# A fourth buffer for the gate matrices of the last layer's experts

## The chip, the cores and the metric

The kernel runs on one core of a Trainium2 chip. The metric is the device time of one execution in microseconds (us). The kernel before took 1708.57 us, the median of 3 runs (1705.90, 1708.57 and 1712.19).

## What is computed

A backbone of two layers over 256 latent tokens and 256 context tokens, of 1024 numbers each, all in float32. Each layer does: a normed and modulated input, three token mixers from one projection, a merge, an output projection, a residual; then the mixture of experts, which is where the change is:

```python
def grouped_moe(h, router_w, router_b, w_gate, w_up, w_down):
    ...                                   # top 2 of 16 experts for each token
    for e in range(N_EXPERTS):            # 16
        he = jax.nn.silu(h @ w_gate[e]) * (h @ w_up[e])
        out = out + combine[..., e:e + 1] * (he @ w_down[e])
    return out
```

`w_gate[e]` and `w_up[e]` are 1024 by 512, `w_down[e]` is 512 by 1024: 2 MB each, 6 MB for an expert, 96 MB for a layer, and each is used once. The last layer (layer 1) works on the 256 latent tokens alone.

## The kernel before, in words

The kernel gives each expert its tokens: the router's choice becomes lists of tokens, the rows of an expert's tokens are gathered from a copy of the tokens in HBM (`moe_rows`), turned, multiplied by gate and up, turned again, multiplied by down. In the last layer each expert has room for 64 tokens in the main loop, and the results are summed by TensorE in PSUM. An expert of the last layer has these steps on TensorE, in this order for expert i: its gate product (L1361, 32 matmuls), the sum of expert i-2's results (L1404), the turn of expert i-1's hidden rows (L1369), its up product (L1361, 32 matmuls), the turn of expert i+1's rows (L1351), the turn of a table of weights (L1394), and the down product of expert i-1 (L1379, 16 matmuls).

**Where the matrices go.** Each of the three matrices has a small set of buffers ("ways") in the on-chip memory. `WAYS[l]` (line 52) is how many for gate, up and down in layer l: 3, 3 and 3 in the last layer. Expert i's matrix uses buffer i modulo the count. Buffer 0 is a slot of the `ring` of weights, the others are pieces of other tensors (`more_sets`, line 389): for gate in the last layer, buffer 1 is half of `residual` and half of `ret_tab`, buffer 2 is `hT`. `expert_parts` (line 783) gives the pieces of a buffer and `expert_tile` (line 839) issues one DMA for each piece. A gate or up matrix has 16 KB in a row for each of 128 partitions, so a piece of a quarter has rows of 4 KB.

**What sets the order.** SyncE (SP) issues all weight transfers from one queue, in the order of its program. In the last layer it first issues the matrices of experts 0, 1 and 2 at places fixed by hand; then the loop at line 958 runs over the experts: for step i it waits until expert i's gate product is done and issues the gate of expert i + 3, waits for expert i's up product and issues the up of expert i + 3, waits for expert i-1's down product and issues the down of expert i + 2. The order in the queue is therefore gate, up, down, gate, up, down. After the loop SP issues the final gain row.

GpSimd has its own queue: a gather of the first experts' rows (L2400), four small scatters that write the lists of tokens (`slot_tokens`, L2422, 12 in the whole kernel with the eight of the first layer), a read of the lists, and then a gather for each expert.

The pieces of memory named by the change are parts of `arena`, a tensor that many stages share: columns 12288 and 13312 hold the tokens' rows `h_tok` that the product `first_rows` reads to make the first expert's rows (it ends by raising `moe.rowsT`), 7168 a modulation row, 18432 tables of the router.

Of the kernel before, what the change touches and what calls it, by code (L numbers as in the profile page):

```python
# [17 lines left out]
ALU = mybir.AluOpType  # L18
# [7 lines left out]
D = 1024  # L26
# [15 lines left out]
EXPERTS = 16  # L42
# [5 lines left out]
TILE = KD * COLS  # L48
CAPS = ((P,) * 4 + (96,) * 6 + (64,) * 6, (64,) * EXPERTS)
RUN = ((0, 1, 10, 2, 4, 11, 3, 12, 5, 6, 7, 8, 9, 13, 14, 15), tuple(range(EXPERTS)))  # L50
FIXED = 2
WAYS = ((3, 3, 2), (3, 3, 3))
CHIP = (3, EXPERTS)
POOL_TILES = 2
MARK_IN = 4
# [62 lines left out]
def first_tile(l):  # L118

    return 0 if l < DEPTH - 1 else XT  # L120
# [129 lines left out]
def trunk(nc, x, c, ctx, c_ctx, w_ada, b_ada, norm_mix_g, norm_ffn_g, w_in, diff_lambda, diff_subln_g,  # L250
# [22 lines left out]
    with ExitStack() as stack:  # L273
        def sb(name, cols, dt=F32):
            return stack.enter_context(nc.sbuf_tensor(name, [P, cols], dt))

        def sem(name):
            return stack.enter_context(nc.semaphore(name))


        res_flat = sb("residual", NT * D)[:, :]
        res = res_flat.rearrange("p (t d) -> p t d", t=NT)
        hT_flat = sb("hT", KD * TOK)[:, :]
# [3 lines left out]
        ret_flat = sb("ret_tab", RT_H * 2 * TAB)[:, :]  # L287
# [3 lines left out]
        NCOL = DEPTH + DEPTH * KB  # L291
        p_col = sb("p_col", NCOL)
# [46 lines left out]
        def region(at, n):  # L339
            assert at + n <= ARENA  # L340
            return arena[:, at:at + n]
# [31 lines left out]
        def mod_rows(l, g, n=1):  # L373
# [13 lines left out]
        junk2 = region(17920, 512).bitcast(BF16)  # L387
        big = lambda at: [region(at, 2 * TILE)]
        more_sets = (([big(20992), [hT_flat]], [big(3072), [region(16384, TILE), ret_flat[:, 0:TILE]]], [big(7168)]),
                     ([[res_flat[:, 0:TILE], ret_flat[:, 0:TILE]], [hT_flat]], [big(8192), big(3072)], [big(20992), big(14336)]))  # L390

        rows_e, rowsT_of = region(0, D), (chunks(1024, KD, P), chunks(1024, KD, MORE))
        y_bufs = ((region(2048, D), region(11264, D)), (region(2048, 512), region(2560, 512)))
# [23 lines left out]
        PC_SUB, PC_GN = 0, DEPTH  # L417
# [4 lines left out]
        param_in, x_in, const_in, ret_in = sem("param_in"), sem("x_in"), sem("const_in"), sem("ret_in")  # L422
        ctx_in, gains_in = sem("ctx_in"), sem("gains_in")
        slot_in = [sem(f"slot{s}_in") for s in range(RING)]
        expert_in = [[sem(f"expert_{name}{way}_in") for name in ("gate", "up", "down")] for way in range(max(max(w) for w in WAYS))]
        ada_ready = sem("ada_ready")
        ident_in, cond_in, bias_in = sem("ident_in"), sem("cond_in"), [sem(f"bias{n}_in") for n in range(4)]
        rows_zeroed, mods_row = sem("rows_zeroed"), sem("mods_row_ready")
        eps_set = sem("eps_set")
        cols_turned, cols_kept, cols_scaled = sem("cols_turned"), sem("cols_kept"), sem("cols_scaled")  # L430
        cond_ready, lam_ready = sem("cond_ready"), sem("lam_ready")
        lam_exp, gam_ready = sem("lam_exp"), sem("gam_ready")
        mods_a = sem("mods_a_ready")
# [15 lines left out]
        h2_ready, h2_out, h2_turned = sem("h2_ready"), sem("h2_out"), sem("h2_turned")  # L449
# [12 lines left out]
        moe = Moe(sem, "moe")  # L462
# [4 lines left out]
        nq = [NT - first_tile(l) for l in range(DEPTH)]  # L467
# [8 lines left out]
        def before(counts, l):  # L476
            return sum(counts[:l])
# [242 lines left out]
        def multiplied(key):  # L720
# [9 lines left out]
            if kind == "out":  # L730
                return wo_ready, 2 * before(nq, l + 1)
            return (moe.gate, moe.up, moe.down)[j], EXPERTS * l + max(i for i in range(EXPERTS) if i % WAYS[l][j] == 0) + 1

# [49 lines left out]
        def expert_parts(l, i, j):  # L783

            k = KF if j == 2 else KD
            if i % WAYS[l][j] == 0:
                return [expert_slot(expert_slots[l][j], k)]
            parts = more_sets[l][j][i % WAYS[l][j] - 1]
            return [part.rearrange("p (k c) -> p k c", k=k // len(parts)) for part in parts]
# [4 lines left out]
        def weights_in(l, i, j):  # L794
            same = lambda m, upto: sum(len(expert_parts(m, n, j)) for n in range(upto) if n % WAYS[m][j] == i % WAYS[l][j])
            return 16 * (sum(same(m, EXPERTS) for m in range(l)) + same(l, i + 1))
# [23 lines left out]
        def _(sp):  # L820
# [20 lines left out]
            def expert_tile(l, i, j, e):  # L841

                at = 0
                for part in expert_parts(l, i, j):
                    k = part.shape[1]
                    if j == 2 and in_pairs(cap_of(l, i)):
                        to, of = part.rearrange("p (h j) c -> p h (j c)", j=2), pairs_v[l, e][:, at // 2:(at + k) // 2, :]
                    else:
                        to, of = part, (gate_v, up_v, down_v)[j][l, e][:, at:at + k, :]
                    sp.dma_start(to, of).then_inc(expert_in[i % WAYS[l][j]][j], 16)  # L850
                    at += k
# [21 lines left out]
            for l in range(DEPTH):  # L873
# [80 lines left out]
                chosen = {2: expert_of(2)}  # L954
                expert_tile(l, 2, 0, chosen[2])
                if l == 0:
                    expert_tile(l, 2, 1, chosen[2])
                for i in range(EXPERTS):
                    ahead, later = i + WAYS[l][0], i - 1 + WAYS[l][2]
                    if ahead < EXPERTS:  # L960
                        chosen[ahead] = expert_of(ahead)
                        sp.wait_ge(moe.gate, EXPERTS * l + i + 1)
                        expert_tile(l, ahead, 0, chosen[ahead])
                        sp.wait_ge(moe.up, EXPERTS * l + i + 1)
                        expert_tile(l, ahead, 1, chosen[ahead])
                    if i >= 1 and later < EXPERTS:
                        sp.wait_ge(moe.down, EXPERTS * l + i)
                        expert_tile(l, later, 2, chosen.pop(later))
# [524 lines left out]
        def _(act):  # L1493
# [45 lines left out]
            for l in range(DEPTH):  # L1539
# [96 lines left out]
                def keep_o(b, j):  # L1636
                    act.wait_ge(o_turned, 2 * KB * l + KB * (b == 0) + j + 1)
                    bank = bank_of(l, banked[l].index(("turn_o", j))) if b == 2 else 2 + j
                    src, dst = ps[:, bank, P * t0:TOK], oT[b][:, j, P * t0:TOK]
                    if (l, b, j) == (0, 2, 0):  # L1640
                        act.wait_ge(cols_scaled, 1)
                    if b == 2:
                        ins = act.activation(dst, src, ACT.Copy, scale=p_col[:, PC_GN + KB * l + j:PC_GN + KB * l + j + 1])  # L1643
                    else:
                        ins = act.activation(dst, src, ACT.Copy, scale=p_col[:, PC_SUB + l:PC_SUB + l + 1])
                    ins.then_inc(oT_ready, 1)
# [147 lines left out]
        def _(dve):  # L1794
# [6 lines left out]
            def mixers_constants():  # L1801

                dve.wait_ge(const_in, 16)
                dve.tensor_copy(tri_ones[:, :], cst[:, C_TRI:C_TRI + 2 * P + 2 * NT])
                dve.wait_ge(param_in, 16 * PARAMS)
                lv = lam_in.rearrange("p (n a d) -> p n a d", a=2, d=HD)
                lt = lam_t.rearrange("p (n d) -> p n d", d=HD)
                step(dve.tensor_tensor(lt, lv[:, :, 0, :], lv[:, :, 1, :], ALU.mult))
                step(dve.tensor_reduce(lam[:, 0:4], lt, AX.X, ALU.add))

                dve.scalar_tensor_tensor(out=lgwork[:, 0, :], in0=loggam[:, :], scalar=-1.0, in1=loggam[:, :],
                                         op0=ALU.mult, op1=ALU.min).then_inc(lam_ready, 1)
                dve.wait_ge(lam_exp, 2)
                for l in range(DEPTH):
                    init = 0.8 - 0.6 * math.exp(-0.3 * l)
                    dve.scalar_tensor_tensor(out=lam[:, 8 + l:9 + l], in0=lam[:, 5 + 2 * l:6 + 2 * l], scalar=-init,
                                             in1=lam[:, 4 + 2 * l:5 + 2 * l], op0=ALU.add, op1=ALU.subtract)

                e_, s_, s2, acc = (lgwork[:, i, :] for i in (1, 2, 3, 0))
                step(dve.tensor_scalar(s_, e_, 2.0, None, ALU.add))  # L1820
                step(dve.reciprocal(s_, s_))
                step(dve.tensor_tensor(s_, s_, e_, ALU.mult))
                step(dve.tensor_tensor(s2, s_, s_, ALU.mult))
                step(dve.tensor_scalar(acc, s2, 1.0 / 17, None, ALU.mult))
                for n in range(7, 0, -1):
                    step(dve.scalar_tensor_tensor(out=acc, in0=acc, scalar=1.0 / (2 * n + 1), in1=s2,
                                                  op0=ALU.add, op1=ALU.mult))
                step(dve.scalar_tensor_tensor(out=acc, in0=acc, scalar=1.0, in1=s_, op0=ALU.add, op1=ALU.mult))
                step(dve.tensor_scalar(acc, acc, 2.0, None, ALU.mult))
                dve.scalar_tensor_tensor(out=loggam[:, :], in0=loggam[:, :], scalar=0.0, in1=acc,  # L1830
                                         op0=ALU.min, op1=ALU.subtract).then_inc(gam_ready, 1)
                dve.wait_ge(cols_kept, 1)
                for l in range(DEPTH):
                    init = 0.8 - 0.6 * math.exp(-0.3 * l)
                    step(dve.tensor_scalar(p_col[:, PC_SUB + l:PC_SUB + l + 1], p_col[:, PC_SUB + l:PC_SUB + l + 1],
                                           0.5 * (1.0 - init), None, ALU.mult))
                dve.tensor_scalar(p_col[:, PC_GN:NCOL], p_col[:, PC_GN:NCOL], 0.5, None, ALU.mult).then_inc(cols_scaled, 1)

            def modulation(l, g):

# [35 lines left out]
            for l in range(DEPTH):  # L1876
# [298 lines left out]
                at = 0  # L2175
# [326 lines left out]
```

## Time and profile before

| | us |
|---|---|
| median of 3 runs | 1708.57 |
| lowest, highest | 1705.90, 1712.19 |
| the profiled execution | 1709.88 |
| its span | 1708.2 |
| TensorE busy in the span | 1618.7 (95%) |
| VectorE, ScalarE busy | 522.2, 316.2 |
| mean granted TensorE clock | 0.985 of full speed |
| moved by DMA | 370.52 MB, mean 217 GB/s |

The profile is of one execution; the durations below are from it. A busy share is a mean over the whole span: what bounds the last layer's experts must be read from their own stretch, which starts near 1460 us (the first gate product) and ends near 1700 us. The DMA share of a stretch is the mean over 16 DMA engines.

### The profile page before, as it was taken

What the parts mean: (1) busy time and instruction counts of PE and PEld (TensorE: products, weight loads), DVE (VectorE), ACT (ScalarE), POOL (GpSimd) and SP (SyncE); (2) the same over time, 40 slices, a digit from 0 to 9 for tenths busy, and PEclk for the clock granted to TensorE, in tenths of its full rate; (3) what the DMA queues carried; (4) which work ended last, traced back from release to release, by engine and by line L of the source; (5) the groups of instructions that cost most, each with busy time, mean ns of one, the idle gap of its engine ahead of it and who ended that gap; (6) DMA issues with size and microseconds to landing.
All of it is one profiled execution on the core that took longest, in us unless ns stands there. A gap on an engine that the chain in (4) does not pass through costs nothing.

```text
span 1708.2 us, 21387 instructions
## 1 busy us (share of the span) xinstructions
PE 1618.7 (95%) x9005; PEld 988.9 (58%) x9005; DVE 522.2 (31%) x1210; ACT 316.2 (19%) x715; POOL 64.6 (4%) x68
## 2 busy tenths in 40 slices
PE   5999988999999999988999998999999998999987
PEld 2765634744444436854546655776678887555543
DVE  1232365522433112431111115345534314211112
ACT  2121233211111100110011013234312201100001
POOL 0000000000000000020000013000000000100000
PEclk8999999999999999999999999999999999999999
DMA  9463412233424447289999995432124366999996
GB/s 371 185 222 148 148 37 83 55 112 104 156 91 168 159 144 287 81 214 396 408 391 392 400 357 204 136 99 74 38 75 147 117 236 267 346 389 392 395 386 267
DMA packets 118863, 370.52 MB, mean 217 GB/s; under 512 B 6722, under 2 KB 83580, under 8 KB 96236
## 3 DMA queue, kind: packets, MB, share of 16 engines
q1 hardware_dynamic: 109516, 344.70, 54.8%
q0 software_dynamic: 4400, 13.69, 2.4%
q10 hardware_dynamic: 4848, 10.73, 2.0%
q8 instruction: 73, 1.20, 0.3%
q14 instruction: 26, 0.21, 0.0%
HBM read 356.40 MB, written 12.69 MB: 216 GB/s over the span
## 4 chain that ended last, share of the span: by engine, by line
PE 81%; DMA 8%; DVE 4%; SPq 2%; ACT 2%; POOL 1%; issue 1%; ACTq 0%; DVEq 0%; POOLq 0%
PE ps L1221 15%; PE ps L1361 12%; PE ps L1094 11%; PE ps L1097 9%; PE ps L1018 8%; PE ps L1238 7%; PE ps L1379 6%; PE ps L1031 3%; DMA ring<-in_w_exp_gate 3%; SPq L850 2%; PE ps L1129 1%; DMA arena<-moe_rows,idx_all 1%; PE ps L1124 1%; PE ps L1351 1%; PE ps L1404 1%; PE ps L1147 1%
## 5 line engine op out<-in xcount | busy, mean ns | idle before, releaser
L1221 PE MATMUL ps<-hT,ring 128*128 128x512 f32 (+1 forms) x768 | 262.3, 491 | 1.4 <-ACT arena L1643 1.4
L1094 PE MATMUL ps<-hT,ring 128*128 128x512 f32 (+1 forms) x544 | 209.7, 538 | 0.0
L1221 PEld LDWEIGHTS ps<-hT,ring 128*128 128x128 f32 x768 | 142.5, 190 | 115.2 <-issue 105.8
L1097 PE MATMUL ps<-ring,hT 128*128 128x256 f32 (+1 forms) x832 | 175.3, 368 | 5.1 <-DVE arena L1919 4.0
L1097 PEld LDWEIGHTS ps<-ring,hT 128*128 128x128 f32 x832 | 148.0, 192 | 36.1 <-issue 18.6
L1094 PEld LDWEIGHTS ps<-hT,ring 128*128 128x128 f32 x544 | 101.2, 191 | 97.7 <-issue 92.7
L1238 PE MATMUL ps<-arena,ring 128*128 128x512 f32 (+1 forms) x384 | 133.4, 487 | 0.0
L1361 PE MATMUL ps<-ring,arena 128*64 128x256 f32 (+2 forms) x928 | 117.1, 377 | 5.6 <-DMA ring<-in_w_exp_gate 3.1
L1361 PE MATMUL ps<-arena 128*64 128x256 f32 (+2 forms) x1008 | 99.6, 355 | 3.8 <-DMA arena<-in_w_exp_up 2.7
L1238 PEld LDWEIGHTS ps<-arena,ring 128*128 128x128 f32 x384 | 72.3, 190 | 51.5 <-issue 46.7
L1361 PEld LDWEIGHTS ps<-ring,arena 128*64 128x64 f32 (+2 forms) x928 | 67.3, 136 | 53.1 <-issue 34.1
L1018 PE MATMUL ps<-ring,arena 128*128 128x256 f32 x384 | 84.3, 381 | 1.6 <-DVE arena L2088 1.5
L1361 PEld LDWEIGHTS ps<-arena 128*64 128x64 f32 (+2 forms) x1008 | 60.8, 130 | 37.5 <-issue 16.9
L1018 PEld LDWEIGHTS ps<-ring,arena 128*128 128x128 f32 x384 | 72.5, 190 | 13.4 <-DVE arena L2088 2.8
L1379 PE MATMUL ps<-arena 128*64 128x512 f32 (+2 forms) x352 | 76.3, 558 | 4.0 <-issue 2.6
L1611 ACT ACTIVATE arena<-ps,st 128x512 f32<-128x512 f32 (+1 forms) x96 | 58.2, 612 | 81.5 <-DVE st L1981 44.3
L1379 PE MATMUL ps<-ring,arena 128*64 128x512 f32 (+2 forms) x352 | 66.4, 522 | 0.2 <-issue 0.2
L2087 DVE SCALAR_TENSOR_TENSOR arena<-arena,ps 128x512 f32<-128x512 f32 (+1 forms) x32 | 17.7, 555 | 154.4 <-PE ps L1238 154.4
L2283 DVE COPY arena<-ps 128x256 f32<-128x256 f32 (+2 forms) x32 | 15.4, 482 | 159.4 <-PE ps L1369 159.4
L1031 PE MATMUL ps<-ring,cond 128*32 128x512 f32 x384 | 55.3, 669 | 9.3 <-DMA ring<-in_w_ada 7.3
L2293 DVE TENSOR_TENSOR arena<-arena,ps 128x256 f32<-128x256 f32 (+2 forms) x32 | 20.9, 653 | 141.4 <-PE ps L1361 141.4
L1652 ACT ACTIVATE arena<-ps 128x512 f32<-128x512 f32 (+1 forms) x48 | 23.5, 490 | 219.0 <-PE ps L1221 219.0
(258 smaller groups left out, 1535.4 us busy)
## 6 DMA issues: line engine op xcount, KB each, us to landing
ring<-in_w_in SPq DMA_DIRECT2D x54, 1024.0 KB, 6.2
ring<-in_w_ada SPq DMA_DIRECT2D x48, 1024.0 KB, 7.1
arena<-in_w_exp_down SPq DMA_DIRECT2D x18, 2048.0 KB, 23.9
arena<-in_w_exp_up SPq DMA_DIRECT2D x15, 2048.0 KB, 24.2
ring<-in_w_exp_down SPq DMA_DIRECT2D x14, 2048.0 KB, 20.7
ring<-in_w_exp_gate SPq DMA_DIRECT2D x12, 2048.0 KB, 23.6
ring<-in_w_exp_up SPq DMA_DIRECT2D x12, 2048.0 KB, 23.8
hT<-in_w_exp_gate SPq DMA_DIRECT2D x10, 2048.0 KB, 22.6
```

The costliest lines, as they stand in the source:

```text
L850: sp.dma_start(to, of).then_inc(expert_in[i % WAYS[l][j]][j], 16)
L1018: last = pe.matmul(dst, a, b, start=(i == 0), stop=(i == len(pairs) - 1))
L1031: last = pe.matmul(ps[32 * c:32 * (c + 1), 7, :], cond[:, k, :], slot(n)[:, 512 * c:512 * (c + 1)], start=(k == 0), stop=(k == KD - 1))
L1094: last = pe.matmul(ps[:, bank, 0:tok.stop - tok.start], w[:, k, at:at + width], hT[:, k, tok], start=(k == 0), stop=(k == KD - 1))
L1097: last = pe.matmul(ps[:, bank, 0:width], hT[:, k, P * tok:P * (tok + 1)], w[:, k, at:at + width], start=(k == 0), stop=(k == KD - 1))
L1221: last = pe.matmul(ps[:, 0, lo:TOK], kview(n)[:, k, P * (m % 2):P * (m % 2 + 1)], hT[:, k, lo:TOK], start=(k == 0), stop=(k == KD - 1))
L1238: last = pe.matmul(ps[:, 1, lo:TOK], wide(n)[:, k, P * (m % 2):P * (m % 2 + 1)], oT[BRANCH_ORDER[b_n]][:, k, lo:TOK], start=(k == 0), stop ...
L1361: last = pe.matmul(ps[wid * i:wid * (i + 1), bank, col:col + cols], rowsT_of[l][:, j, at:at + wid], w[j][:, cols * i:cols * (i + 1)], star ...
L1379: last = pe.matmul(ps[wid * i:wid * (i + 1), Y_AT[l] + p + half, 0:cols], hidT_of[l][:, block, wid * side:wid * (side + 1)], w[j][:, cols ...
L1611: ins = act.activation(prob[:, g % 2, 512 * j:512 * j + nk], ps[:, 2 + j, 0:nk], ACT.Exp, bias=s[:, 2 + j:3 + j], scale=SCALE, accum_out=s ...
L1652: act.activation(sig[:, v % 2, P * t0:TOK], ps[:, 0, P * t0:TOK], ACT.Tanh, scale=0.5).then_inc(sig_ready, 1)
L2293: return dve.tensor_tensor(out, a, b, ALU.mult)
```

## The change

`WAYS` for the last layer goes from (3, 3, 3) to (4, 3, 3). A fourth gate buffer is made of four pieces of 1024 columns of `arena`. Before the loop SP waits until all tokens' rows are ready and until the first expert's rows are made, and issues expert 3's gate as four DMAs of 512 KB. In the loop the gate that is issued is that of expert i + 4, and the up has its own counter (`above`, expert i + 3 as before). One semaphore (`cols_scaled`) is joined with another (`cols_kept`), and the list of the weights' semaphores has a fourth entry for gate alone. Experts 3, 7, 11 and 15 use the new buffer, 1, 5, 9 and 13 the one in two pieces.

```diff
-WAYS = ((3, 3, 2), (3, 3, 3))
+WAYS = ((3, 3, 2), (4, 3, 3))
...
-                     ([[res_flat[:, 0:TILE], ret_flat[:, 0:TILE]], [hT_flat]], [big(8192), big(3072)], [big(20992), big(14336)]))
+                     ([[res_flat[:, 0:TILE], ret_flat[:, 0:TILE]], [hT_flat], [region(at, D) for at in (12288, 13312, 7168, 18432)]], [big(8192), big(3072)], [big(20992), big(14336)]))
...
+                if WAYS[l][0] > 3:
+                    sp.wait_ge(h2_ready, before(nq, l + 1))
+                    sp.wait_ge(moe.rowsT, EXPERTS * l + 1)
+                    chosen[3] = expert_of(3)
+                    expert_tile(l, 3, 0, chosen[3])
                 for i in range(EXPERTS):
-                    ahead, later = i + WAYS[l][0], i - 1 + WAYS[l][2]
+                    ahead, above, later = i + WAYS[l][0], i + WAYS[l][1], i - 1 + WAYS[l][2]
                     if ahead < EXPERTS:
                         chosen[ahead] = expert_of(ahead)
                         sp.wait_ge(moe.gate, EXPERTS * l + i + 1)
                         expert_tile(l, ahead, 0, chosen[ahead])
+                    if above < EXPERTS:
                         sp.wait_ge(moe.up, EXPERTS * l + i + 1)
-                        expert_tile(l, ahead, 1, chosen[ahead])
+                        expert_tile(l, above, 1, chosen[above])
                     if i >= 1 and later < EXPERTS:
                         sp.wait_ge(moe.down, EXPERTS * l + i)
                         expert_tile(l, later, 2, chosen.pop(later))
...
-                        act.wait_ge(cols_scaled, 1)
+                        act.wait_ge(cols_kept, 2)
...
-                dve.tensor_scalar(p_col[:, PC_GN:NCOL], p_col[:, PC_GN:NCOL], 0.5, None, ALU.mult).then_inc(cols_scaled, 1)
+                dve.tensor_scalar(p_col[:, PC_GN:NCOL], p_col[:, PC_GN:NCOL], 0.5, None, ALU.mult).then_inc(cols_kept, 1)
```

## Rows read from the trace of the kernel before

**Rows 1.** Page, 40 equal slices of the span: busy tenths of TensorE and the DMA engines.

```profile
PE   5999988999999999988999998999999998999987
DMA  9463412233424447289999995432124366999996
```

**Rows 2.** Stretches: length, busy us of PE, PEld, DVE, ACT, POOL, PEclk, DMA share, GB/s.

```profile
1460.00:1609.00 149.00, 147.11 (x1064) 77.12 (x1064) 24.01 (x53) 15.06 (x34) 12.25 (x14) 0.99 1.01 379
1609.00:1693.00 84.00, 72.64 (x502) 40.77 (x502) 12.38 (x27) 5.79 (x14) 2.66 (x3) 1.00 0.97 382
```

**Rows 3.** Chain that ended last, from 1633 us: start us, us, what.

```profile
1633.70 43.22 DMA ring<-in_w_exp_gate
1677.05 3.67 PE ps L1361 x32
```

**Rows 4.** Timeline of SP's issues, experts 14 and 15: start us, us, engine, line, out<-in.

```profile
1626.17 4.83 SPq L850 DMA_DIRECT2D arena<-in_w_exp_up  x1
1631.05 2.60 SPq L850 DMA_DIRECT2D arena<-in_w_exp_down  x1
...
1638.08 3.07 SPq L850 DMA_DIRECT2D ring<-in_w_exp_up  x1
...
1659.14 0.38 SPq L850 DMA_DIRECT2D ring<-in_w_exp_down  x1
```

**Rows 5.** DMA issues, us to landing last: those issued at 1626.17, 1631.05, 1633.70, 1638.08.

```profile
arena<-in_w_exp_up SPq DMA_DIRECT2D x1, 2048.0 KB, 40.9
...
arena<-in_w_exp_down SPq DMA_DIRECT2D x1, 2048.0 KB, 41.0
...
ring<-in_w_exp_gate SPq DMA_DIRECT2D x1, 2048.0 KB, 43.2
...
ring<-in_w_exp_up SPq DMA_DIRECT2D x1, 2048.0 KB, 43.7
```

**Rows 6.** Timeline of TensorE, experts 14 and 15; in brackets idle before and its end.

```profile
1667.18 3.67 PE L1361 MATMUL ps<-arena 128*64 128x256 f32 x32 [0.45 <-DMA arena<-in_w_exp_up]
...
1672.11 3.65 PE L1379 MATMUL ps<-arena 128*64 128x512 f32 x16 [0.25 <-issue]
...
1682.94 3.67 PE L1361 MATMUL ps<-ring,arena 128*64 128x256 f32 x32
```

**Rows 7.** Timeline of SP's issues at the start: expert 2's gate, expert 3's gate and up.

```profile
1447.04 0.33 SPq L850 DMA_DIRECT2D hT<-in_w_exp_gate  x1
1465.44 0.33 SPq L850 DMA_DIRECT2D ring<-in_w_exp_gate  x1
1469.59 0.33 SPq L850 DMA_DIRECT2D ring<-in_w_exp_up  x1
```

**Rows 8.** DMA issues: us to landing of the issues at 1447.04, 1465.44, and an earlier one at 1435.60.

```profile
hT<-in_w_exp_gate SPq DMA_DIRECT2D x1, 2048.0 KB, 21.6
...
ring<-in_w_exp_gate SPq DMA_DIRECT2D x1, 2048.0 KB, 14.2
...
ring<-in_w_exp_up SPq DMA_DIRECT2D x1, 2048.0 KB, 7.5
```

**Rows 9.** Stretches as in rows 2: both layers' list scatters, and just after the last layer's.

```profile
1466.00:1476.00 10.00, 9.20 (x84) 5.75 (x86) 1.45 (x4) 0.98 (x2) 0.59 (x1) 1.00 1.00 175
1476.00:1486.00 10.00, 10.00 (x80) 5.44 (x78) 1.91 (x4) 0.87 (x2) 0.93 (x1) 1.00 1.00 410
750.00:766.00 16.00, 15.10 (x42) 7.01 (x41) 1.90 (x4) 1.19 (x2) 4.52 (x6) 1.00 0.99 154
```

**Rows 10.** DMA by size of packet, 930 to 940 us: first layer, many 4 KB rows.

```profile
DMA packets 646, 3.91 MB, mean 391 GB/s; under 512 B 58, under 2 KB 58, under 8 KB 510
```

**Rows 11.** Page, DMA issues: pieces of 512 KB, and the gate matrices in two pieces.

```profile
ring<-in_w_branch SPq DMA_DIRECT2D x24, 512.0 KB, 3.6
...
residual<-in_w_exp_gate SPq DMA_DIRECT2D x5, 1024.0 KB, 23.8
ret_tab<-in_w_exp_gate SPq DMA_DIRECT2D x5, 1024.0 KB, 27.5
```

More of the change, by code:

```diff
@@ L424, in trunk @@
         slot_in = [sem(f"slot{s}_in") for s in range(RING)]
-        expert_in = [[sem(f"expert_{name}{way}_in") for name in ("gate", "up", "down")] for way in range(max(max(w) for w in WAYS))]
+        expert_in = [[sem(f"expert_{name}{way}_in") for name in ("gate", "up", "down")[0:sum(max(w[j] for w in WAYS) > way for j in range(3))]]
+                     for way in range(max(max(w) for w in WAYS))]
         ada_ready = sem("ada_ready")
@@ L429, in trunk @@
         eps_set = sem("eps_set")
-        cols_turned, cols_kept, cols_scaled = sem("cols_turned"), sem("cols_kept"), sem("cols_scaled")
+        cols_turned, cols_kept = sem("cols_turned"), sem("cols_kept_and_scaled")
         cond_ready, lam_ready = sem("cond_ready"), sem("lam_ready")
```

## The prediction, made before the change was run

> **What bounds the kernel now.** I read the slices of the page first, then stretches of the last layer's experts, then the chain of waits, and last the single transfers. The slices show TensorE near full nearly everywhere, and two places where the DMA engines are full too: the experts of the two layers [rows 1]. For the last layer the stretches split in two. From 1460 to 1609 us TensorE works 147.1 of 149 us; from 1609 to 1693 it works 72.6 of 84, so 11.4 us are idle, while the DMA share stays near 1 in both [rows 2]. TensorE is ahead of the transfers at the start, loses that lead and then waits. The chain says the same: it goes through the transfer of the last gate, issued at 1633.70 and landed 43.2 us later, to the gate product at 1677.05 [rows 3, 5]. A transfer of 2 MB that lands 43 us after its issue is not short of a buffer. 43.2 us at 390 GB/s are 16.8 MB, or eight matrices ahead of it in the queue.
>
> An expert brings 6 MB, 6.29 million bytes, 16.1 us at the 390 GB/s that I take from rows 10 (391). TensorE needs about 14.0: 5.89 us from a gate product to its up product (1677.05 to 1682.94, no idle), 4.6 to 4.7 from there to the down product (1667.18 to 1672.11, less 0.25 of idle), and 3.5 for that [rows 3, 6]. So the queue is the bound, by some 2.1 us an expert, and what counts is when each place in the queue lands, and which product waits for which place.
>
> **The change part by part.**
>
> *The earlier issue.* Expert 3's gate now goes out when the first expert's rows are made, just before the first gate product at about 1460, in place of 1465.44 [rows 7]. But the transfer before it, expert 2's gate, was issued at 1447.04 and lands 21.6 us later, at 1468.64 [rows 7, 8]. The queue isn't empty in between, so the early issue moves no byte forward. It would, if the queue ran dry after 1468.6, and there the trace has something odd: 175 GB/s from 1466 to 1476 against 410 in the next 10 us [rows 9]. That is 2.35 MB missing, 5.7 us of transfer. Is it a lack of work? Expert 3's gate was issued at 1465.44 and needs 14.2 us, where one alone took 7.5 [rows 8]. It was in the queue all that time and crawled. The same slump stands in the first layer from 750 to 766 us, 154 GB/s, also just behind the list scatters [rows 9]: 256 GB/s missing for 16 us is 4.1 MB, or 10.0 us at 410, for eight scatters, 1.25 each; the last layer has four and lost 5.7, 1.4 each. A price for each scatter explains both. The bounds are 0 and -5.7 us. I take -0.4, near the difference between the two prices over four scatters (0.6), since a single matrix in the queue may have left a little undone.
>
> *The order in the queue.* This is what the change really moves. Before, the end of the queue is gate 14, up 14, down 13, gate 15, up 15, down 14, down 15. Gates now come one expert, three places, earlier in the program, and each up and down of the middle slips back by one place for the gate that was put in front of them. The end becomes gate 15, up 14, down 13, up 15, down 14, down 15. All are 2 MB, so a place lands when it landed before. From rows 4 and 5: up 14 at 1626.17 + 40.9 = 1667.07; down 13 at 1631.05 + 41.0 = 1672.05; gate 15 at 1633.70 + 43.2 = 1676.90; up 15 at 1638.08 + 43.7 = 1681.78. With the change the place of 1667.07 carries gate 15, that of 1672.05 up 14, that of 1676.90 down 13, and up 15 keeps 1681.78.
>
> TensorE's order is unchanged: up 14, down 13, gate 15, up 15. Up 14 starts at about 1672.2 in place of 1667.18. Down 13 comes 4.6 to 4.9 us behind an up product (1667.18 to 1672.11, with 0.25 us of idle) [rows 6], so at about 1677.0, when its matrix lands too. It takes some 3.5 us (3.65 in rows 6, less the overlap with what follows). Gate 15 starts at 1680.5, long landed. In the profile before, gate 15 to up 15 is 1677.05 to 1682.94, 5.89 us [rows 3, 6]; so up 15 starts at 1680.5 + 5.9 = 1686.4. It was 1682.94: 3.5 us later. Its matrix (1681.78) is no longer the wait, and from up 15 to the end nothing changes: +3.5 us. In short: when the matrix of 1676.90 lands, a gate product was left to do before up 15; now a down product and the gate product are. The prefetched gate is early by over 10 us, and its place was paid for by matrices that are needed sooner.
>
> The price rests on SP issuing in time. Up 15 now waits behind the wait for up 12's product, which comes one place of the queue, some 5 us, later than before (1643 in place of 1638.08), as does each down. Down 15 was issued at 1659.14 and now goes out at about 1664 [rows 4], when down 12's product is done; five matrices, some 25 us, are still ahead of it. So these delays cost 0 with that cover; without it each would cost its 5 us. What stands behind SP's new wait for the first rows is only the loop's own wait for the first gate product: 0.
>
> *Four pieces in place of one.* Experts 3, 7, 11 and 15 take four DMAs of 512 KB with rows of 4 KB. Against the buffers before that is 12 DMAs more and one less for the two-piece buffer, which now serves one expert fewer: 11. In the first layer a stretch in which 510 of 646 packets are under 8 KB runs at 391 GB/s [rows 10], the same as here, so short rows cost 0. For a DMA more: the two halves of a two-piece gate land 3.7 + 0.4 us apart by their medians (27.5 against 23.8, and issued about 0.4 later) [rows 11], and 1 MB at 390 takes 2.7. Medians over two layers' loads are rough; I take bounds of 0 and 0.3 us each for a queue that never empties, 0 to 3.3 us together, and the value 0.3 us in all, since the full queue hides what is fixed in a DMA. The outer bound is that of an empty queue: pieces of 512 KB land 3.6 us after issue there [rows 11], 14.4 for four, against 7.5 for a 2 MB alone [rows 8]: 6.9 us more, 28 for four matrices.
>
> The Trainium skill speaks against exactly this: "DMA: Bandwidth & Descriptors", in the section on bandwidth, asks for DMAs of at least 1 MiB to reach three quarters of peak, and its fit gives each a fixed 2.0 us. An estimate from that page, if the fixed part were not hidden, is 11 times 2.0, 22 us slower. This case's transfers overlap in the queue (land after land about 5 us apart with 2 MB each, rows 4 and 5), which bears out that a fixed part is hidden while there is a backlog.
>
> *Semaphores.* ScalarE's wait for `cols_kept` at 2 is met by the same VectorE instruction as before: 0.
>
> Sum: 3.5 for the order, -0.4 for the early issue, +0.3 for the pieces: 3.4 us. The profiled execution took 1709.88, so 1713.3; it lies 1.3 above the median of 1708.57, so the median I predict is **1712.0 us**, +0.2%. A measurement of this kernel can't tell less than about 0.5%, 8.5 us, from no change, so this is "same" by that bound.
>
> **The rivals.**
>
> *The slump is filled (faster).* If the DMA engines at 1466 to 1476 lacked other work to switch to, the early gate fills all 5.7 us, and every later place lands earlier: 3.5 + 0.3 - 5.7 = -1.9, time 1706.7. For it: only one or two matrices were outstanding there. Against it: the first layer's slump. 15%.
>
> *The order doesn't matter (no change).* If matrices don't land place by place, since engines share several DMAs, down 13 may land with gate 15's old neighbours and the 3.5 us vanish: 1708.6. Against it: landings of rows 5 lie 4.9 to 5.0 us apart, in order. 13%.
>
> *The pieces cost (slower).* This decides if a DMA in the full queue has a price of its own above 0.5 us. At 0.3 us each: 3.5 + 3.3 = 6.8, 1715.4, 13%. At the price of an empty queue: 3.5 + 28 = 31, 1740; it needs a queue without backlog, which isn't there: 3%.
>
> My own forecast, the order's price: 56%.
>
> **How the numbers follow.** The range goes from the filled slump (1706.7) to the pieces at 0.3 us with about 1.5 us of scatter between medians: 1706.5 to 1717. Faster by over 0.5% needs 8.5 us, more than the filled slump gives: 3%. Slower by over 0.5%: the 3% of the last case, and half of the 13%, if the pieces cost a bit more: 9%. Same: 88%.
>
> **What would show it.** Right: in the changed profile the first waits of TensorE for a matrix come earlier than 1609, near 1587 (expert 9), and are at the up products, some 2 us for each expert, and at the down products; gate products wait for nothing, and gate 15 lands 10 us or more before its use; up 15 starts 3 to 4 us later; 1466 to 1476 stays near 175 GB/s; the last gate is no longer in the chain, an up or a down is. Wrong: places 2 or 3 land well before 1480 and the whole queue ends before 1688 (the slump was filled), or the queue runs under 385 GB/s from 1500 on (the pieces cost).

## The result

The changed kernel takes 1712.57 us (median of 20 runs, 1709.86 to 1716.44); the kernel before takes 1708.87 us over its own 20 (1705.90 to 1714.41). The ratio is 1.0020, 95% interval [1.0012, 1.0029]: +3.4 us by the ratio and +3.7 by the medians, slower, and within the 0.5% that the prediction counts as the same. The forecast was 1712.0.

The profiled execution of the changed kernel has the same span as the one before, 1708.2 us. That is no sign of no change. What comes ahead of the edit was 3.6 us shorter in this execution, from small differences in stages that the edit leaves alone. So the last layer must be read from a mark of its own. I take the issue of the first expert's up matrix, the first transfer behind the empty stretch of the queue: 1435.60 before, 1432.02 after. From it to the end the kernel before needs 272.6 us and the changed one 276.2: +3.6. (Below, up 14 is the up matrix of expert 14, or the product that uses it; gate and down likewise.)

The stretches of rows 2 in the changed kernel (columns as there):

```profile
1460.00:1609.00 149.00, 143.26 (x1036) 76.97 (x1034) 23.39 (x51) 13.20 (x32) 8.70 (x10) 0.98 1.01 381
1609.00:1693.00 84.00, 76.19 (x518) 41.55 (x514) 13.05 (x29) 6.13 (x16) 3.55 (x4) 0.98 0.93 364
```

The queue moves as much as before in the first stretch (381 and 379 GB/s) [rows 2]; in the second it is done earlier by the 3.6 us of the shift. TensorE is now idle in the first too. Its timeline shows where; the bracket is the idle time ahead of an instruction and what ended it:

```profile
1583.50 3.67 PE L1368 MATMUL ps<-ring,arena 128*64 128x256 f32 x32 [0.45 <-DMA ring<-in_w_exp_up]
...
1601.58 6.21 PE L1368 MATMUL ps<-arena 128*64 128x256 f32 x32 [3.90 <-DMA arena<-in_w_exp_up]
...
1634.67 3.67 PE L1368 MATMUL ps<-ring,arena 128*64 128x256 f32 x32 [2.29 <-DMA ring<-in_w_exp_up]
...
1651.72 5.04 PE L1368 MATMUL ps<-arena 128*64 128x256 f32 x32 [2.75 <-DMA arena<-in_w_exp_up]
...
1668.76 3.67 PE L1368 MATMUL ps<-arena 128*64 128x256 f32 x32 [1.66 <-DMA arena<-in_w_exp_up]
...
1673.65 3.65 PE L1386 MATMUL ps<-arena 128*64 128x512 f32 x16 [0.21 <-issue]
1677.11 3.65 PE L1368 MATMUL ps<-arena 128*64 128x256 f32 x32
...
1682.97 3.67 PE L1368 MATMUL ps<-ring,arena 128*64 128x256 f32 x32
```

The line at 1583.50 is the up product of expert 9, the first to wait; then come those of experts 10, 12, 13 and 14. The one of expert 11 has no such wait. No gate product waits for its matrix any more. Expert 15's gate product (1677.11) follows down 13 at once, and up 15 starts at 1682.97. From the mark that is 250.95 us, 247.34 before: +3.6, and from there to the end both take the same 25.2 to 25.3 us.

SP's issues of the same matrices, and the time to landing of two of them, issued at 1633.90 (up 14) and 1640.05 (up 15):

```profile
1618.52 15.34 SPq L851 DMA_DIRECT2D arena<-in_w_exp_gate  x4
1633.90 2.44 SPq L851 DMA_DIRECT2D arena<-in_w_exp_up  x1
...
1640.05 12.30 SPq L851 DMA_DIRECT2D ring<-in_w_exp_up  x1
```

```profile
arena<-in_w_exp_up SPq DMA_DIRECT2D x1, 2048.0 KB, 34.7
...
ring<-in_w_exp_up SPq DMA_DIRECT2D x1, 2048.0 KB, 38.5
```

Up 15 lands at 1678.55 and is used at 1682.97, 4.42 us later. In the kernel before it landed at 1681.78 and was used at 1682.94, 1.16 us later [rows 4 to 6]. I call this the lag: how far TensorE is behind the queue at the last up product. The queue brought up 15 at 246.5 us from the mark, 246.2 before. So the transfers took no longer; TensorE had 3.3 us more left to do when this matrix landed.

The chain of waits tells the same: the last gate is gone from it, up 14 stands there (start us, us, what).

```profile
1633.90 34.72 DMA arena<-in_w_exp_up
1668.62 0.14 issue
1668.76 3.67 PE ps L1368 x32
```

### The profile page after: what moved, and what is told of

It reads as the page before. It is cut to its first block, busy times and chain, and to the rows that moved or that the text cites. A ratio compares the mean times of both kernels' runs of the same rounds, so it can differ in the third digit from the quotient of the medians.

```text
span 1708.2 us, 21399 instructions
## 1 busy us (share of the span) xinstructions
PE 1621.5 (95%) x9005; PEld 989.5 (58%) x9005; DVE 522.1 (31%) x1210; ACT 316.5 (19%) x715; POOL 64.7 (4%) x68
## 4 chain that ended last, share of the span: by engine, by line
PE 79%; DMA 9%; DVE 4%; SPq 2%; ACT 2%; POOL 1%; issue 1%; ACTq 0%; DVEq 0%; POOLq 0%
PE ps L1228 15%; PE ps L1368 11%; PE ps L1101 11%; PE ps L1104 9%; PE ps L1025 8%; PE ps L1245 7%; PE ps L1386 6%; DMA arena<-in_w_exp_up 4%; PE ps L1038 3%; SPq L851 2%; PE ps L1136 1%; DMA arena<-moe_rows,idx_all 1%; PE ps L1131 1%; PE ps L1154 1%; PE ps L1358 1%
## 5 line engine op out<-in xcount | busy, mean ns | idle before, releaser
L1368 PE MATMUL ps<-arena 128*64 128x256 f32 (+2 forms) x1136 | 118.1, 366 | 9.4 <-DMA arena<-in_w_exp_up 8.3
L1368 PE MATMUL ps<-ring,arena 128*64 128x256 f32 (+2 forms) x864 | 110.1, 378 | 4.7 <-DMA ring<-in_w_exp_up 2.7
L1368 PEld LDWEIGHTS ps<-arena 128*64 128x64 f32 (+2 forms) x1136 | 72.5, 134 | 51.0 <-issue 27.7
L1368 PEld LDWEIGHTS ps<-ring,arena 128*64 128x64 f32 (+2 forms) x864 | 63.0, 137 | 48.6 <-issue 31.8
```

The lines of the kernel that those rows point to most:

```text
L1368: last = pe.matmul(ps[wid * i:wid * (i + 1), bank, col:col + cols], rowsT_of[l][:, j, at:at + wid], w[j][:, cols * i:cols * (i + 1)], star ...
```

## The experiments

All times are against runs of the kernel before on the same chip, which change a little from one group of runs to the next; so ratios are compared, and 0.001 is 1.7 us. A difference in us behind a ratio is worked out from the ratio. It is not exactly that of the medians: the two lie up to 0.0011, 1.8 us, apart here, so a difference below 2 us is uncertain even in its sign.

### Is it the order? Four kernels

**Gates last, with the fourth buffer.** In the last layer each gate is issued behind the up and the down of its step.

```diff
-                    if ahead < EXPERTS:
+                    if l == 0 and ahead < EXPERTS:
...
                     if i >= 1 and later < EXPERTS:
                         sp.wait_ge(moe.down, EXPERTS * l + i)
                         expert_tile(l, later, 2, chosen.pop(later))
+                    if l == 1 and ahead < EXPERTS:
+                        chosen[ahead] = expert_of(ahead)
+                        sp.wait_ge(moe.gate, EXPERTS * l + i + 1)
+                        expert_tile(l, ahead, 0, chosen[ahead])
```

> The changed kernel with its fourth gate buffer and its early first issue, but in the last layer's loop each gate goes out behind the up and the down of its step, so that the order in the queue is that of the kernel before. If the order in the queue is the price (my theory), this gives back what the change lost: 1708.6 to 1709.6, 0 to +1 us against before, gate 15 lands behind down 13, up 15 starts as before. If the buffer itself, its four pieces or the early issue beside the list scatters are the price, it stays at about 1712.5, +3.7.

Measured: 1706.88 us, ratio 0.9988 [0.9978, 0.9998]. All of the loss is gone. (The same code measured again for the square below gave 1.0002 [0.9993, 1.0011]: as fast as before, not faster.) Up 15 was issued at 1647.61 and landed 35.2 us later, at 1682.81, and its product starts at 1683.95: a lag of 1.14 us, as before the change.

```profile
1678.06 3.67 PE L1372 MATMUL ps<-arena 128*64 128x256 f32 x32 [1.42 <-DMA arena<-in_w_exp_gate]
...
1683.95 3.67 PE L1372 MATMUL ps<-ring,arena 128*64 128x256 f32 x32
```

```profile
ring<-in_w_exp_up SPq DMA_DIRECT2D x1, 2048.0 KB, 35.2
```

The gate product waits again, for the fourth buffer this time, and the kernel is as fast as the one before. The buffer isn't what costs.

**The order alone, with three buffers.** The kernel before, with up and down of the last layer issued one step later.

```diff
-                        sp.wait_ge(moe.up, EXPERTS * l + i + 1)
-                        expert_tile(l, ahead, 1, chosen[ahead])
-                    if i >= 1 and later < EXPERTS:
-                        sp.wait_ge(moe.down, EXPERTS * l + i)
+                    above, freed = ahead - l, i + 1 - l
+                    if 3 <= above < EXPERTS:
+                        sp.wait_ge(moe.up, EXPERTS * l + freed)
+                        expert_tile(l, above, 1, chosen[above])
+                    later, freed = later - l, i - l
+                    if freed >= 1 and later < EXPERTS:
+                        sp.wait_ge(moe.down, EXPERTS * l + freed)
```

> The kernel before with its three gate buffers, none in four pieces, but each up and down of the last layer's loop is issued one step later, so that the queue carries the order of the changed kernel: gate 15, up 14, down 13, up 15, down 14, down 15 at its end. If the order is the price: +3.5 us against before, 1712. If the buffer or its pieces are: 0. One matrix fewer is outstanding at the start, which costs up to 1 us more if the queue runs dry near 1475 to 1490.

Measured: 1713.26 us, ratio 1.0032 [1.0019, 1.0046], +5.5 us. The loss appears with no fourth buffer at all. Up 15, issued at 1641.34, lands at 1681.14 and is used at 1685.59: a lag of 4.45 us. So the order accounts for 3.3 us here. The rest of the 5.5 isn't explained: the matrix landed 248.8 us from the mark, 2.6 later than before; the matrix fewer at the start may be a part of that, or the difference between executions.

```profile
1685.59 3.67 PE L1364 MATMUL ps<-ring,arena 128*64 128x256 f32 x32
```

```profile
ring<-in_w_exp_up SPq DMA_DIRECT2D x1, 2048.0 KB, 39.8
```

**Only the last gate moved back.** The condition of the first edit is `(l, ahead) != (1, EXPERTS - 1)` at the first place and `==` at the second, so that gate 15 alone goes behind up 14 and down 13.

> The changed kernel, in which the gate of expert 15 alone goes out behind up 14 and down 13; all other gates stay ahead. If only what is left to do behind the last matrices counts, as my sum has it, the waits at the up products of experts 9 to 13 stay and yet the whole 3.5 us come back: 1709, 0 to +1 against before. If waits add up over the experts, it stays near +3 us.

Measured: 1707.84 us, ratio 1.0008 [0.9995, 1.0021], +1.4 us, -0.9 to +3.6. By the times alone the +3 us of waits that add up isn't excluded. The profile decides it as far as one execution can: the waits in the middle stand, and from the mark to the end this kernel needs 273.4 us, with 272.6 before and 276.2 with all gates ahead. Most of the loss is gone:

```profile
1650.86 3.67 PE L1372 MATMUL ps<-arena 128*64 128x256 f32 x32 [2.54 <-DMA arena<-in_w_exp_up]
...
1679.01 3.67 PE L1372 MATMUL ps<-ring,arena 128*64 128x256 f32 x32
```

The last wait for a matrix is at the up product of expert 13. From there TensorE runs two experts, up to the start of up 15, in 28.15 us without another, and that is now the bound. The waits of single experts do not add up in the time; what counts is the work that is left behind the last of them. The profile has no landing for up 15 here, so this kernel has no lag.

**Pieces.** The kernel before with its second and third gate buffers in four pieces each.

```diff
-[[res_flat[:, 0:TILE], ret_flat[:, 0:TILE]], [hT_flat]]
+[[t[:, D * q:D * (q + 1)] for t in (res_flat, ret_flat) for q in range(2)], [hT_flat[:, D * q:D * (q + 1)] for q in range(4)]]
```

> The kernel before, with its second and third gate buffers loaded in four pieces of 512 KB each (they were two of 1 MB and one of 2 MB): 25 DMAs more in the last layer, same bytes, same order. At no price for a DMA in a full queue: 0 to +1 us. At the upper bound of the prediction, 0.3 us each: +7.5, 1716. At a fixed 2 us each: +50.

Measured: 1709.11 us, ratio 1.0005 [0.9994, 1.0015]. 25 DMAs more cost 0.9 us, -1.0 to +2.6: at most 0.1 us each. For the 11 of the change that is 0.4 us, at most 1.1. A price of 2 us each would have shown as 50: whatever is fixed in a DMA was hidden in this full queue.

### The early issue, the scatters, and a byte moved ahead

**Gates last, first issue late.** As gates last, but expert 3's gate waits for `moe.gate` in place of `moe.rowsT`.

> The kernel with gates last in each step (order of before, fourth buffer), but expert 3's gate waits for the first gate product, as in the kernel before, 6 us later. It differs from that kernel by the early issue alone. My theory (the queue isn't empty when the early issue comes, the slump behind the list scatters is their own price): no difference to it, 0 to +1 us, and so 1707 to 1709 here. The rival (the slump is a lack of work that the early matrix fills): up to 5.7 us slower than it, 1712.

Measured: 1709.82 us, ratio 1.0009 [0.9999, 1.0019], +1.5 us (the median is 0.3 below that of the kernel before). Against its partner, gates last with the early issue, that is 3.6 us, between my two theories, but the partner's 0.9988 is from another group of runs. This called for the square below.

**Four more scatters.**

```diff
+                    if l == 1 and i == 3:
+                        for t in range(nq[l]):
+                            for j in range(2):
+                                pool.indirect_dma_start(out=spare_d, in_=tok_i[:, t0 + t:t0 + t + 1], in_offset=None,
+                                                        out_offset=bass.IndirectOffsetOnAxis(
+                                                            ap=dest_i[:, 2 * t + j:2 * t + j + 1], axis=0)).then_inc(spared, 16)
```

> The kernel before with four more scatters of 128 words each in the last layer, into a spare tensor that nobody reads, issued behind expert 3's gather near 1482 us, where two matrices and more are outstanding and nothing else waits for GpSimd. If a scatter takes its own time from the transfers (1.25 to 1.4 us each, my reading of the slump), a second slump appears and the end comes 5 to 5.6 us later, 1714. If the slump was a lack of queued work: 0 to +1 us.

Measured: 1715.42 us, ratio 1.0031 [1.0019, 1.0043]: +5.3 us, 1.3 us a scatter (0.8 to 1.8). Stretches of this kernel and, below, of the kernel before (columns as in rows 2; the last number is GB/s):

```profile
1484.00:1500.00 16.00, 14.38 (x92) 6.89 (x90) 1.78 (x5) 1.25 (x3) 5.86 (x6) 0.89 1.00 283
```

```profile
1484.00:1500.00 16.00, 16.00 (x122) 8.65 (x120) 2.44 (x6) 1.25 (x3) 0.97 (x1) 1.00 1.02 381
```

98 GB/s less for 16 us are 1.6 MB, 4 us at 390, while the DMA share stays at 1.00. At least three matrices were outstanding all the time (the last of them, issued at 1483.39, 1486.84 and 1492.73, landed at 1505.1, 1510.9 and 1515.8). TensorE lost time here too, as the gather issued just ahead of the scatters came 1.62 us late and the next down product took 5.35 us in place of 3.65; but with so much outstanding that didn't starve the queue. So a scatter of 128 words took its time out of the transfers even behind a backlog.

**One quarter early.** Gates last; the first piece of the fourth buffer is the last third of `ret_tab`, issued at about 1406 behind expert 1's down.

```diff
-[region(at, D) for at in (12288, 13312, 7168, 18432)]
+[ret_flat[:, 2 * D:3 * D]] + [region(at, D) for at in (12288, 13312, 7168)]
...
                 expert_tile(l, 1, 0 if l == 0 else 2, 1)
+                if l == 1:
+                    expert_tile(l, 3, 0, 3, 0, 1)
```

The new arguments take the first piece alone; the other three go out where all four did.

> The kernel with gates last in each step, and the first quarter of the fourth buffer in the last third of ret_tab, which is dead since the retention stage, so that 512 KB of expert 3's gate are issued at about 1408, into the stretch 1422 to 1436 in which the queue of the kernel before is empty. If the experts of the last layer are bound by the bytes in the queue, each byte moved ahead of 1436 counts: 0.52 MB at 390 GB/s, -1.3 us against the kernel with gates last, about 1705.5. If a lead of the transfers is no gain (TensorE bound, or the queue empty elsewhere): 0.

Measured: 1707.23 us against 1710.11 in its group, ratio 0.9985 [0.9976, 0.9994], -2.6 us. In its group it is faster than the kernel before. The step over gates last alone can't be told: that measured 0.9988 and, again, 1.0002, each in another group, so the step is 0.5 or 2.9 us, with some 2 us of uncertainty.

**Two quarters early.** And the first quarter of expert 2's up.

> As the one with one quarter early, and the first quarter of expert 2's up matrix as well (its buffer in four pieces, the first of them in columns that are dead since the first branch): 1 MB moved into the empty stretch, -2.7 us against the kernel with gates last, about 1704.2, -4.4 against before. If bytes in the queue are not the bound: 0.

Measured: 1708.07 us, ratio 0.9986 [0.9975, 0.9998], -2.4 us. The forecast of -4.4 lies just outside the interval (-4.3 to -0.3): the second quarter brought nothing that the times show. The single profile leans the other way: up 15 lands 244.45 us from the mark, 245.9 with one quarter, 246.2 in the kernel before. One execution each, and the same figure is 248.5 and 249.3 in two executions of gates last. So this is open.

### A square: order by first issue

The last four stand beside each other on one chip, so that the terms can be told apart.

> One corner of a square of order (gates ahead or last) by first issue (early or late), all four corners beside each other: gates last, early issue, the same code as in the first of these experiments. Theory A, the terms of the prediction (order +3.5, early issue -0.4, pieces +0.3): 0 to -0.1 us against before. Theory B, from the runs so far (order about +5.5, early issue about -3): -2 us.

> Second corner: gates last, late issue. Theory A: +0.3 us against before. Theory B: +1 to +1.5.

> Third corner: the changed kernel, gates ahead, but expert 3's gate is issued behind the first gate product, some 6 us later. Theory A: +3.8 us against before. Theory B: +6 to +7.

> Fourth corner: the changed kernel itself. Theory A: +3.4 us against before, and 3.5 above gates last with early issue. Theory B: +3.5 too, but 5.5 above gates last with early issue.

| | gates last | gates ahead |
|---|---|---|
| early issue | 1710.62 us, 1.0002 [0.9993, 1.0011] | 1714.86 us, 1.0025 [1.0016, 1.0034] |
| late issue | 1712.42 us, 1.0009 [1.0000, 1.0018] | 1715.10 us, 1.0035 [1.0021, 1.0048] |

The order costs 0.0023 and 0.0026, 3.9 and 4.4 us; the early issue gives 0.0007 and 0.0010, 1.2 and 1.7 us, each with 2 to 3 us of uncertainty. So the order is clear of the noise, and the early issue isn't. Theory A had 3.5 and 0.4, theory B 5.5 and 3. The times lie between them, nearer to A.

The lag decides what the times leave loose, as it doesn't depend on how fast the queue was in an execution. It is the start of the last up product less the landing of its matrix, from one profile each:

```
gates last:  before 1.16  e1 1.14  pieces 1.13  e5 1.16  one quarter 1.09  two 1.11  scatters 1.07  square 1.16, 1.07
gates ahead: after 4.42   order only 4.45   square 4.51, 4.55
```

(e1 is gates last, e5 the same with the late issue.) Two groups with nothing between them, whatever buffers and pieces there are: the order costs 3.4 us (the means differ by that, single pairs by 3.3 to 3.5). What differs beside it is the landing itself, 246.2 to 250.1 us from the mark without added scatters or early quarters. This moves by more than the early issue or the pieces could, and one profile can't tell them.

## Why the prediction was right

- **The queue is the bound, not the number of buffers.** Right. The change added a buffer and the queue's rate stayed. From 1500 us on, the sign that I had named, it is 390 GB/s to 1688 us, and 392 over the same stretch from the mark before. 0.5 MB moved into the empty stretch came with one of the two lowest ratios (0.9985), though its own share isn't separated.
- **The order, +3.5.** Right as mechanism and place: the order alone, with three buffers, brings the loss, and its undoing with four buffers takes it away. The size is 3.4 by the lag, 3.9 and 4.4 by times with wider intervals. The steps of the sum came true one by one, with the shift of 3.6 added: up 14 at 1672.3 (forecast 1672.2), down 13 at 1677.2 (1677.0), gate 15 at 1680.7 (1680.5), up 15 at 1686.6 (1686.4). The places of the waits were right too: first at expert 9's up product, forecast near 1587, seen at 1583.50, which is 1587.1 with the shift of 3.6. The waits that the forecast put at the down products too did not come: those stand still only 0.2 us, and not for a DMA. Gate 15's own landing isn't in the profile; it went out ahead of up 14, which landed 8.5 us before gate 15 was used.
- **The early issue, -0.4.** The sign is likely right, and the size is open. The square says -1.2 and -1.7, neither clear of its noise, and the pair from two groups -3.6. The slump wasn't filled: from 1462 to 1472, the same stretch from the mark, the changed kernel moves 227 GB/s. The 175 of before [rows 9] is one execution, though: over the same 10 us from the mark the kernels with the late issue moved between 122 (gates last, late issue, first of its two runs) and 256 GB/s (the order alone). In the one with 122 the DMA share of the stretch is 0.63, 1.00 in the kernel before: there the engines did lack work for a part of the time. So neither the 5.7 us that the prediction read from the slump nor a gain read from it is firm. That the scatters can own the greater part of it is borne out by the run with four more: 1.3 us each, 0.8 to 1.8, forecast 1.25 to 1.4.
- **The pieces, +0.3.** 0.4 by experiment, -0.4 to +1.1. The rival of 0.3 us a piece does not hold in a full queue: 25 would have been +7.5 us. The Trainium skill's page "DMA: Bandwidth & Descriptors" (section "Anatomy of one DMA — SWDGE (gpsimd) path") gives a DMA issued from GpSimd a fixed 2.0 us; these are issued from SP. An estimate at that page's price would have been +50 us, and the 0.9 us measured shows that no such part adds up here.
- **SP's later issues, 0.** Right for landing: down 15, issued at 1661.40, lands at 1688.30, 256.3 us from the mark, 256.1 before.
- With the order at 3.4, the early issue at -1.2 to -1.7 and the pieces at 0.4 the sum would be 2.1 to 2.6, and 3.4 was measured, 2.1 to 5.0 by its interval. So nothing has to be missing. The late corner of gates last has +1.5 us in both of its measurements (1.0009), with the order and the first issue of the kernel before; but each interval reaches down to 1, and the medians there say -0.3 and +2.5. This hints at a small cost of the fourth buffer beside its gains, of which the four-piece DMAs would be a part; it isn't shown. That the total came out at the forecast's 3.4 is luck in part: its two small terms are known to no better than 1 or 2 us each, and errors in them may have cancelled. What is shown is the large term.

## What to carry to other kernels

When a transfer queue is full to the end, as this one was, a further buffer for one operand brings no byte forward; it only lets that operand overtake others, which then are late. Compare, matrix by matrix, what is left to compute when each lands, and keep the queue in the order of use; the last few transfers set the time. Where bytes can be moved forward is where the queue is empty and memory is dead; what that is worth isn't settled here (one quarter -2.6 us, two -2.4, against the kernel before, and gates last alone measured -2.1 and +0.3).

## What the runs showed that was not expected

**A wait can be followed by a product at half the clock.** After 3.90 us of idle the up product of expert 10 took 6.21 us in place of 3.67, and after 2.75 us that of expert 13 took 5.04. The granted clock in these stretches (next to last but one column) is the lower of the two levels (1.2 and 2.4 GHz) for all or part of the time:

```profile
1600.00:1605.00 5.00, 3.42 (x16) 2.17 (x18) 0.00 (x0) 0.00 (x0) 0.00 (x0) 0.50 1.04 434
1650.00:1655.00 5.00, 3.28 (x18) 2.21 (x20) 0.00 (x0) 0.00 (x0) 0.00 (x0) 0.66 1.00 410
```

Idle time alone doesn't tell: the order-only kernel waited 3.06 us and its product took 3.67, and gates last waited 2.54 and its product took 5.36. Here the loss of 1.4 to 2.5 us was covered, since TensorE still waited for a later matrix (2.29 us at up 12, 1.66 at up 14). Behind the last wait nothing would cover it; no run here had that.

**The backlog seems to shrink with small pieces.** SP spent 15.34 us to issue the four pieces of gate 15, where 0.33 us is usual for a DMA with room in the queue [rows 7]. A matrix in one piece can block it too: up 15 took 12.30 us to issue. Up 14 landed 34.7 us after its issue, 40.9 before [rows 5], so fewer bytes were ahead of it. The queue may take a number of pieces and not of bytes; no run separates that. It cost nothing here, since the queue never ran empty.
